# Sums of half a dense block kept in one PSUM bank, three banks in turn for the rest, and one gathered row in the short pairs

## The reference

```
u = take(expert_down, e_idx)                    # (t, h, k, 1024)
act = gelu(einsum('td,thkd->thk', hb, u))
wv = gates * act
y = einsum('thk,thkd->td', wv, take(expert_up, e_idx))
out = rms_norm(x + y, g_final)
```

## Time and profile before

| what | value |
|---|---|
| three executions | 3024.17, 3027.0, 3028.58 us; median 3027.0 |
| the profiled execution | 3019.19 us |
| its span | 3017.4 us |
| mean granted TensorE clock | 0.972 of full speed |

### The profile page before, as it was taken

The page is one execution under the profiler, slowest core; times in us unless marked ns, Lnnn a source line. Parts: engine busy times, 40 slices in busy tenths (PEclk is TensorE's granted clock), DMA queues, the critical chain, the costliest instruction groups (busy, mean ns, idle before and its releaser), DMA issues.

```text
span 3017.4 us, 40171 instructions
## 1 busy us (share of the span) xinstructions
PE 2844.6 (94%) x15235; PEld 2477.6 (82%) x15235; DVE 2336.3 (77%) x4348; ACT 937.1 (31%) x1356; POOL 2124.3 (70%) x1552
## 2 busy tenths in 40 slices
PE   7999898999899799899999998999999989999996
PEld 6678777677689688889998997899899979989995
DVE  1332298345499899588999999898899979889998
ACT  4232433232332399322222222222222222222221
POOL 4324576338568799778887886888688868878883
PEclk9899999899899899999999999999999999999998
DMA  3112412112322377989998997999899979989996
GB/s 140 43 63 91 168 64 70 42 50 98 112 87 94 120 238 237 332 310 330 347 349 315 342 336 289 335 342 341 311 343 336 346 266 339 348 311 341 335 337 219
DMA packets 267584, 717.92 MB, mean 238 GB/s; under 512 B 20864, under 2 KB 104064, under 8 KB 267392
## 3 DMA queue, kind: packets, MB, share of 16 engines
q0 software_dynamic: 110912, 403.75, 35.8%
q1 hardware_dynamic: 156480, 311.61, 30.6%
HBM read 657.86 MB, written 57.41 MB: 237 GB/s over the span
## 4 chain that ended last, share of the span: by engine, by line
PE 34%; DVE 8%; POOL 7%; DMA 6%; issue 3%; ACT 1%; DVEq 0%; SPq 0%; ACTq 0%
PE abank L1530 6%; PE abank L1532 6%; PE abank L1531 6%; PE ybank L1546 6%; PE ybank L1547 5%; PE ybank L1548 5%; POOL up L1475 3%; DVE acc L1684 3%; DMA up<-in_down,e_idx 3%; POOL tdown_lo L1482 2%; DMA up<-in_up,e_idx 2%; DVE up L1672 2%; DVE e_y L1731 1%; POOL tup_lo L1486 1%; DMA w<-all_pre 1%
## 5 line engine op out<-in xcount | busy, mean ns | idle before, releaser
L1530 PE MATMUL abank<-m_hT,tdown_hi 128*128 128x384 f32 (+1 forms) x1856 | 576.4, 311 | 15.0 <-ACT w L1588 9.0
L817 POOL TENSOR_TENSOR m_wlo<-m_raw,m_whi 128x1024 fp32r<-128x1024 f32 x128 | 309.5, 2425 | 379.9 <-ACT m_whi L622 376.7
L1532 PE MATMUL abank<-m_hT,tdown_lo 128*128 128x384 f32 (+1 forms) x1856 | 575.9, 310 | 0.0
L1531 PE MATMUL abank<-m_hlo,tdown_hi 128*128 128x384 f32 (+1 forms) x1856 | 574.9, 310 | 0.0
L1546 PE MATMUL ybank<-tup_hi,w_hi 128*128 128x512 f32 x1280 | 509.1, 398 | 45.5 <-DVE e_y L1731 32.7
L1684 DVE SCALAR_TENSOR_TENSOR acc<-up,e_act,acc 128x1024 f32<-128x1024 f32 x381 | 489.7, 1285 | 65.9 <-DMA up<-in_up,e_idx 43.4
L1672 DVE CUSTOM_DVE_ANT_0 up<-up,acc 128x1024 f32<-128x1024 f32 x384 | 457.0, 1215 | 97.8 <-DMA up<-in_down,e_idx 95.2
L1547 PE MATMUL ybank<-tup_lo,w_hi 128*128 128x512 f32 x1280 | 506.2, 396 | 0.0
L1548 PE MATMUL ybank<-tup_hi,w_lo 128*128 128x512 f32 x1280 | 504.2, 394 | 0.0
L1475 POOL DMA_INDIRECT up<-in_up,e_idx x384 | 396.9, 1033 | 106.0 <-issue 92.4
L1475 POOL DMA_INDIRECT up<-in_down,e_idx x384 | 399.1, 1039 | 99.3 <-issue 88.9
(11 more groups left out here) (226 smaller groups left out, 4714.6 us busy)
## 6 DMA issues: line engine op xcount, KB each, us to landing
e_tup<-in_up SPq DMA_DIRECT2D x128, 512.0 KB
m_raw<-in_tiles SPq DMA_DIRECT2D x116, 512.0 KB, 3.3
e_tdown<-in_downT SPq DMA_DIRECT2D x116, 512.0 KB
gates<-all_table SPq DMA_DIRECT2D x64, 640.0 KB
all_table<-t_out SPq DMA_DIRECT2D x9, 4096.0 KB, 14.7
m_raw<-in_downT SPq DMA_DIRECT2D x12, 512.0 KB, 3.7
up<-in_down,e_idx POOLq DMA_INDIRECT x384
up<-in_up,e_idx POOLq DMA_INDIRECT x384
```

Of the source, the lines that this page charges most:

```text
L1530: nc.tensor.matmul(out, tdown_hi[:, q, at], h2T_hi[:, k, a:b], start=k == 0, stop=False)
L1531: nc.tensor.matmul(out, tdown_hi[:, q, at], h2T_lo[:, a:b, at], start=False, stop=False)
L1532: ins = nc.tensor.matmul(out, tdown_lo[:, q, at], h2T_hi[:, k, a:b], start=False, stop=k == KD - 1)
```

## The change

The half (t = 4, i = 1) of every pair is no longer added to `y` in each pair. Its matmuls go to a bank of its own, `ykept`, with `start` true for the first pair alone, and VectorE adds `ykept` to `y` once, behind the last pair. The other nine halves of a pair take turns in three banks: `turn` numbers them n = 9p + 2t + i, and a half waits for the addition of the half three before it in that numbering. The semaphore `pair_done` counts the kept halves; ScalarE waits for it where it waited for a pair's last `y_ready`. `SHARE` of a short pair becomes 1 in place of 3: five short pairs have one gathered row and one has two, 7 rows in place of 24, and the 17 others go to the other 58 pairs, which have 13 or 14.

```diff
@@ -1280,7 +1280,7 @@
 
 
 
-SHARE = [3 if p + 1 in PRE else 10 for p in range(NPAIR)]
+SHARE = [1 if p + 1 in PRE else 10 for p in range(NPAIR)]
 
 
 def rows_of_pair(p):
@@ -1373,7 +1373,10 @@
             return ctx.enter_context(nc.semaphore(name))
 
         abank = ctx.enter_context(nc.psum_tensor("abank", [P, 2, 512], F32))
-        ybank = [ctx.enter_context(nc.psum_tensor(f"ybank{i}", [P, 512], F32)) for i in range(4)]
+        ybank = [ctx.enter_context(nc.psum_tensor(f"ybank{i}", [P, 512], F32)) for i in range(3)]
+
+
+        ykept = ctx.enter_context(nc.psum_tensor("ykept", [P, 512], F32))
         acc = ctx.enter_context(nc.psum_tensor("acc", [P, D], F32))
         h2_row = acc
 
@@ -1397,6 +1400,11 @@
         w_ready, w_high, w_low = sem("w_ready"), sem("w_high"), sem("w_low")
         y_ready = sem("y_ready")
         y_added = sem("y_added")
+        pair_done = sem("pair_done")
+
+        def turn(p, t, i):
+
+            return None if t == ND - 1 and i == 1 else (2 * ND - 1) * p + 2 * t + i
 
         block = ctx.enter_context(nc.Block())
 
@@ -1537,16 +1545,18 @@
                 if t == 0:
                     pe.wait_ge(w_low, 2 * (p + 1))
                     pe.wait_ge(up_low, 2 * (p + 1))
-                r, n, ts = p % 2, ND * p + t, slice(t * P, (t + 1) * P)
+                r, ts = p % 2, slice(t * P, (t + 1) * P)
                 for i in range(2):
-                    if n >= 2:
-                        pe.wait_ge(y_added, 2 * (n - 2) + i + 1)
-                    out, ds = ybank[n % 2 * 2 + i][:], slice(i * 512, (i + 1) * 512)
+                    n = turn(p, t, i)
+                    if n is not None and n >= 3:
+                        pe.wait_ge(y_added, n - 2)
+                    out, ds = (ykept if n is None else ybank[n % 3])[:], slice(i * 512, (i + 1) * 512)
                     for q in range(2):
-                        nc.tensor.matmul(out, w_hi[r][:, q, ts], tup_hi[r][:, q, ds], start=q == 0, stop=False)
+                        first, last = (q == 0, q == 1) if n is not None else (p + q == 0, p + q == NPAIR)
+                        nc.tensor.matmul(out, w_hi[r][:, q, ts], tup_hi[r][:, q, ds], start=first, stop=False)
                         nc.tensor.matmul(out, w_hi[r][:, q, ts], tup_lo[r][:, q, ds], start=False, stop=False)
-                        ins = nc.tensor.matmul(out, w_lo[r][:, q, ts], tup_hi[r][:, q, ds], start=False, stop=q == 1)
-                    ins.then_inc(y_ready, 1)
+                        ins = nc.tensor.matmul(out, w_lo[r][:, q, ts], tup_hi[r][:, q, ds], start=False, stop=last)
+                    ins.then_inc(pair_done if n is None else y_ready, 1)
 
             for q in range(2):
                 for half in range(2):
@@ -1571,7 +1581,7 @@
             def up_high_of(p, q):
                 act.wait_ge(tup_in[q], 16 * (p + 1))
                 if p >= 2:
-                    act.wait_ge(y_ready, 2 * ND * (p - 1))
+                    act.wait_ge(pair_done, p - 1)
                 if p == 1:
                     act.wait_ge(chunk_out[1], 16 * (NTC // 2))
                 nc.scalar.activation(tup_hi[p % 2][:, q], tup[:, q], ACT.Copy).then_inc(up_high, 1)
@@ -1647,7 +1657,7 @@
                     weights_high(p + 1, 1)
             act.wait_ge(normed, DB)
             for t in range(ND):
-                act.wait_ge(y_added, 2 * (ND * (NPAIR - 1) + t + 1))
+                act.wait_ge(y_added, (2 * ND - 1) * (NPAIR - 1) + 2 * t + 2)
                 if t == 0:
                     act.wait_ge(row_used, NROW)
                 nc.scalar.activation(up[:, t], y[:, t], ACT.Square, accum_out=stat[:, 0, t:t + 1]).then_inc(ssq_ready, 1)
@@ -1724,11 +1734,16 @@
                 nc.vector.tensor_tensor(w_lo[p % 2][:, q], w[:, q], w_hi[p % 2][:, q].bitcast(F32), ALU.subtract).then_inc(w_low, 1)
 
             def add_y(p, t):
-                n = ND * p + t
                 for i in range(2):
-                    dve.wait_ge(y_ready, 2 * n + i + 1)
+                    n = turn(p, t, i)
+                    if n is None and p + 1 < NPAIR:
+                        continue
+                    if n is None:
+                        dve.wait_ge(pair_done, NPAIR)
+                    else:
+                        dve.wait_ge(y_ready, n + 1)
                     part = y[:, t, i * 512:(i + 1) * 512]
-                    nc.vector.tensor_tensor(part, part, ybank[n % 2 * 2 + i][:], ALU.add).then_inc(y_added, 1)
+                    nc.vector.tensor_tensor(part, part, (ykept if n is None else ybank[n % 3])[:], ALU.add).then_inc(y_added, 1)
 
             for q in range(2):
                 weights(0, q)
```

## The result

The changed kernel takes 3040.25 us, the kernel before on the same chip 3026.61 us, medians of eleven executions each. The ratio is 1.0044, with a 95% interval of 1.0034 to 1.0055: slower by 13.6 us. The forecast was 3028 us and no difference. The time lies within the range, but the range was 39 us wide and took in every case but the one of 2989 us; the case that came is the first rival.

A forecast was written before the change was run, and what follows sets the result against it. TensorE was taken to bound the kernel. Short pairs -14, clock -3, three banks +17 and two existing stalls +1 gave +1 us, so 3028 us on the median 3027.0; range 3008 to 3047 us.

The forecast's parts named there:

- the first rival: Waits ahead of block 3's and block 2's second halves: missing bank costs 0.6 us a pair, +18, 3045 us; chance 0.21.
- TensorE is the bound and VectorE's 38 us are worth nothing: Full stretches: TensorE always busy, so 63 fewer additions, 38 us of VectorE, lie beside the path.
- The short pairs give 14 us, and the clock 3: Six short pairs: fewer gathered rows shorten stalls for additions by 14 us; a higher granted clock gives 3 us.
- the two thirds: Short pairs: of at most 20.4 us of stalls that can go, two thirds, 14 us, was taken.
- 17 rows more in the other pairs cost nothing: Other 58 pairs: 0.29 rows more each, covered on VectorE, GpSimd and DMA; nothing taken, upper end 20 us.
- Three banks cost 0.3 us a pair, 17 us, and 1 us for the two stalls: Block 3's second half waits for block 2's first-half addition, 17 us; pair 42 and the last pair add about 1 us.
- Will VectorE be early enough?: Full pairs: VectorE's 0.25 us lead a pair would be swallowed by waits for gathered rows, so the bank wait stays.
- The sum: Whole kernel: -14 - 3 + 17 + 1 = +1 us, 3028 us on the median.
- the main case: Whole kernel: gain and price cancel within 6 us, 3028 us, own range 3021 to 3034; chance 0.38.
- The second rival: Full pairs: the new wait for additions doesn't form; -18, 3009 us; chance 0.27.
- The third: VectorE's additions are the bound, so time falls by 38 us and more, to 2989 us; chance 0.02.
- the fourth: Short pairs: the stall moves from additions to `w_lo`, while the banks cost 17; +15, 3042 us; chance 0.12.

The follow-up runs named there:

- the additions left out: Kernel before, four banks, without adding block 4's second half in 63 of 64 pairs (sums lost): 3023.20 us against 3024.17, ratio 0.9997.
- the bank part alone: Kernel before with one half kept in its own bank and three banks in turn, gathered rows shared as before (SHARE 3): 3048.11 us against 3024.17, ratio 1.0074.
- the moved additions: Changed kernel with the additions of block 1's and block 2's first halves one gathered row earlier: 3014.18 us against 3023.19 before, ratio 0.9979.
- the row part alone: Kernel before with SHARE 1 for a short pair, four banks in turn and all 640 additions: 3019.05 us against 3024.17, ratio 0.9994.

## Where the prediction was right and where it was wrong, step by step

- *TensorE is the bound and VectorE's 38 us are worth nothing.* Right: the additions left out on four banks change nothing, 0.9997.
- *The short pairs give 14 us, and the clock 3.* Right: their sum fell by 18.3 us, clock included, though the two thirds in it was a guess. As said there, TensorE met some of the stalls anew: 21.1 us went ahead of block 4's first half, and 10.5 came back as waits for `w_lo` ahead of the block 0 behind. It takes both parts together to keep three banks from spoiling it: the bank part alone made them 15 us longer.
- *17 rows more in the other pairs cost nothing.* This is one step that failed. Nothing was taken for the rows, since the next term was to contain their effect, but that term, 0.3 us, was read from the trace before, without them. With three banks the row part adds 19.4 us to the others, 11.5 of it ahead of the two halves that wait for late additions. With four banks the cover that was named (VectorE, GpSimd and the DMA engines in a full pair) held in most pairs (27.85 us), and 13.2 us were lost in a few.
- *Three banks cost 0.3 us a pair, 17 us, and 1 us for the two stalls.* This step failed in its size; the mechanism and its place, block 3's second half, were right. The bank part alone costs the other pairs 23 us, and in the changed kernel they lose 42.4. By the starts of the matmuls, TensorE starts 26.6 us later ahead of block 3's second half, 14.0 ahead of block 2's, and loses 10 in these halves themselves; 6.9 are no longer lost ahead of block 4's first half, where pair 42's stall stood, and 5.9 no longer ahead of block 0. I read the lateness against the start of the matmul, 0.22 us in pair 36. But the weight load waits, and it is due one matmul earlier: 0.22 + 0.23 = 0.45 us, and 0.45 us is what the median pair then lost (28.30 - 27.85). That rests on this agreement and on the rows of pair 16; no run tries it by itself. Read so, the same pairs, again without pair 42, give a mean of 0.44 us in place of 0.3, and 25 us for 57 pairs. Besides, I read one wait and not two: block 2's second half waits for block 1's first, and 13 of the 63 pairs lost over 0.1 us there, 15 us in all.
- *Will VectorE be early enough?* Right that it would not: rows were waited for longer, not shorter (180.0 us and not 138.6 over the whole run), and the wait came back in pair after pair until the two additions were moved.
- *The sum.* -17 + 18 became -18 + 42 between the profiles, which overstate the medians' +13.6 by 10 us. With three banks, the row part is worth 9 us (1.0074 to 1.0044, with intervals that don't overlap); with four, nothing that can be told.

The first rival had the right mechanism and sign, and at 0.6 us a pair and 3045 us was 5 us over; its threshold of 0.4 us a pair was passed. It also named the cause that the main case left out, that the added rows push block 2's addition later. The second rival is what the moved additions made true: 3014.18, where it said 3009. The third would have had the time fall with VectorE's work, and the additions left out rule it out; the fourth is wrong too, since the short pairs did give it back.

## What to carry to other kernels

Before a ring of buffers is made shorter, read in the trace, for each user of the ring, when the release that it will then need comes and when its first instruction is due, and on TensorE that is here the weight load, not the matmul. If it is late by tenths of a microsecond on the engine that bounds, move just that release ahead of one piece of other work: here two additions of 0.6 us a pair turned +13.6 us into -9 by the medians. Work freed on an engine off the path pays only once something on the path is rearranged to use it.

## What the runs showed of the hardware

- A wait that ended 0.41 us after a weight load was due, and 0.18 us after its matmul was, held the matmul by 0.24 us and the one behind it by another 0.11 us (pair 16). In 20 of the 43 pairs that lost over 0.1 us ahead of block 3's second half the first delay is 0.22 to 0.25 us. So here a wait cost more than the time it was late at the matmul.
- Short waits hardly show between matmul rows: a 128x512 row lasts 0.39 us at a pace of 0.23, and of pair 16's delay of 0.24 us only 0.08 stands as a gap. The idle time ahead of the weight loads for `ybank` is where they are seen, as in pair 16's rows.
- After TensorE had idled 4.14 us, the granted clock was 0.50 for the next 6 us, and twelve matmuls of a block took about 0.2 us each more than at 1.00 (the row part alone, pair 44).
- The same VectorE instruction, `weights` (128x640, two inputs in SBUF), took between 0.82 and 3.61 us in the changed kernel. GpSimd works in the same time on SBUF, but what of it makes the difference was not tried, and stays open.
